# The LRU recurrence in eight half rounds with the heads of the first attention, and the modulation moved

## The reference

```python
mod_x = (silu_c @ w_mod[l] + b_mod[l])        # six vectors of 1024: sh1, sc1, g1, sh2, sc2, g2
px = modulate(rmsnorm(x, g_pre_mix[l]), sh1, sc1) @ w_in[l]        # q, k, v, lx, zx
...
attn_x = latent_attention(group_q(qx), k_all, v_all)               # 8 heads of 64, 1280 keys
yc, yl = rglru_bidir(dwconv(lc, ...), dwconv(lx, ...), ...)        # linear scans, forward and backward
lru_x = yl * jax.nn.gelu(zx)
mix_x = jnp.concatenate([attn_x, lru_x], axis=-1) @ w_out[l]
x_mid = x + g1 * rmsnorm(mix_x, g_post_mix[l])
hx2 = modulate(rmsnorm(x_mid, g_pre_ffn[l]), sh2, sc2)
ffn_x = peer(hx2, ...)                                             # 128 expert rows of u and of v per token
x = x_mid + g2 * rmsnorm(ffn_x, g_post_ffn[l])
```

## Time and profile before

| | us |
|---|---|
| median of 3 runs (3408.39 to 3414.58) | 3409.09 |
| profiled execution | 3407.63 |
| its span | 3405.9 |
| PE, DVE, ACT, POOL busy | 2665.7, 2199.0, 776.0, 1972.8 |

### The profile page before, as it was taken

The page is one execution under the profiler, slowest core; times in us unless marked ns, Lnnn a source line. Parts: engine busy times, 40 slices in busy tenths (PEclk is TensorE's granted clock), DMA queues, the critical chain, the costliest instruction groups (busy, mean ns, idle before and its releaser), DMA issues.

```text
span 3405.9 us, 29441 instructions
## 1 busy us (share of the span) xinstructions
PE 2665.7 (78%) x9084; PEld 1140.6 (33%) x9084; DVE 2199.0 (65%) x4614; ACT 776.0 (23%) x1791; POOL 1972.8 (58%) x2100
## 2 busy tenths in 40 slices
PE   7998768076977897789778977897789777933498
PEld 3775334053233323332333233323332333211122
DVE  2233961899787677767776777677767866766500
ACT  1122432021222132212221222132213221200122
POOL 0000000257677676767777777777777777777775
PEclk9999988578989898889898989898989889967799
DMA  6002340289999999999999999999999999999998
GB/s 237 31 25 81 136 173 13 96 321 393 387 394 407 395 393 395 405 396 391 403 407 398 395 398 407 400 396 393 407 403 402 407 406 396 386 408 408 406 399 356
DMA packets 326923, 1145.15 MB, mean 336 GB/s; under 512 B 37356, under 2 KB 41452, under 8 KB 325623
## 3 DMA queue, kind: packets, MB, share of 16 engines
q0 software_dynamic: 295552, 1075.97, 80.5%
q1 hardware_dynamic: 31224, 67.38, 5.4%
HBM read 1134.83 MB, written 8.39 MB: 336 GB/s over the span
## 4 chain that ended last, share of the span: by engine, by line
PE 40%; DMA 22%; POOL 15%; DVE 14%; issue 7%; ACT 2%; DVEq 0%; SPq 0%; ACTq 0%; POOLq 0%
PE psum L1446 24%; POOL arena L435 15%; DMA arena<-in_v,arena 11%; DMA arena<-in_u,idx_u 10%; DVE arena L1119 5%; PE psum L1401 4%; PE psum L1271 4%; PE psum L1254 2%; PE psum L1328 2%; PE psum L1367 1%; PE psum L1257 1%; PE psum L1380 1%; PE psum L1220 1%; DVE small L992 1%; DMA arena<-in_w_mod 1%
## 5 line engine op out<-in xcount | busy, mean ns | idle before, releaser
L1446 PE MATMUL psum<-arena 128*32 128x512 f32 x4096 | 1369.6, 675 | 328.0 <-DMA arena<-in_v,arena 320.3
L1119 DVE CUSTOM_DVE_ANT_0 arena<-arena,psum 128x1024 f32<-128x1024 f32 x1024 | 1231.8, 1220 | 515.9 <-DMA arena<-in_u,idx_u 485.4
L435 POOL DMA_INDIRECT arena<-in_u,idx_u x1024 | 967.7, 945 | 440.7 <-issue 225.2
L435 POOL DMA_INDIRECT arena<-in_v,arena x1024 | 984.7, 962 | 358.5 <-issue 210.8
L1446 PEld LDWEIGHTS psum<-arena 128*32 128x32 f32 x4096 | 387.0, 119 | 1252.6 <-issue 1073.3
L688 ACT ACTIVATE arena<-arena 128x32 f32<-128x32 f32 x1024 | 316.9, 320 | 1393.8 <-PE psum L1446 1392.3
L1401 PE MATMUL psum<-wbig,arena 128*128 128x512 f32 x512 | 232.5, 609 | 2.2 <-ACT arena L657 2.2
L1328 PE MATMUL psum<-kT,arena 64*128 64x512 f32 (+1 forms) x384 | 176.6, 599 | 59.3 <-ACT arena L619 39.8
L1348 PE MATMUL psum<-ident,arena 128*128 128x128 f32 x640 | 118.3, 310 | 77.4 <-DVE arena L1006 42.1
L1360 PE MATMUL psum<-arena,v 128*64 128x128 f32 x1280 | 161.0, 283 | 22.7 <-ACT arena L630 22.7
L630 ACT ACTIVATE arena<-psum 128x512 f32<-128x512 f32 (+1 forms) x192 | 99.5, 526 | 263.0 <-PE psum L1348 262.7
(11 more groups left out here) (199 smaller groups left out, 2043.9 us busy)
## 6 DMA issues: line engine op xcount, KB each, us to landing
wbig<-in_w_mod SPq DMA_DIRECT2D x8, 2048.0 KB
arena<-in_u,idx_u POOLq DMA_INDIRECT x1024, 6.7
arena<-in_v,arena POOLq DMA_INDIRECT x1024, 6.7
arena<-in_w_mod SPq DMA_DIRECT2D x4, 2048.0 KB, 10.4
wbig<-in_wq SPq DMA_DIRECT2D x1, 8192.0 KB, 35.5
arena<-in_xin SPq DMA_DIRECT2D x5, 1024.0 KB, 5.0
wbig<-in_w_in SPq DMA_DIRECT2D x2, 2048.0 KB, 23.3
arena<-in_w_out SPq DMA_DIRECT2D x1, 4096.0 KB, 15.3
```

Of the source, the lines that this page charges most:

```text
L435: pool.indirect_dma_start(ring[:, r, :], None, t[table], bass.IndirectOffsetOnAxis(idx[:, j:j + 1], 0)).then_inc(got[r], 16)
L1119: V.tensor_tensor_reduce(ring[:, r, :], ring[:, r, :], hx_cur, 1.0, 0.0, ALU.mult, ALU.add, act_[:, j:j + 1]).then_inc(S["u_used"], 1)
L1446: ins = M(bank(4 + b)[QP * q:QP * q + QP, :], lhsT=sel[:, j % SELS, :], rhs=ring[:, r, 512 * b:512 * b + 512], start=(i == 0), stop=(i == ...
```

## The change

Early modulation: four loads of two row blocks by all 2048 columns, issued at once into four places; PE makes the four blocks of 512 columns in the four column groups of 32 (`sil32`), x's transposes in between; one copy, four transposes, `modc`. The clearing by GpSimd stands ahead and only covers pads of XL. w_in is loaded as three tiles (w_kvl, w_q, w_z), the last two after the early matmuls.

Late modulation: during the projections GpSimd loads w_mod in 32 pieces (128 partitions x 2 x 512), scales each with silu(c) and adds it to `acc` (eight blocks of 512 columns). After the projections PE sums `acc` over partitions with ones, in column groups (`mod_sum`), and DVE updates all four rows at once. `acc` lies where the attention's tiles are later, and partly under what ACT and DVE write in the recurrence, so ACT waits for `mod_out`.

The loops of the projections are written out. The constants of the recurrence are computed after pair 0 and the first convolution in the middle of the last pair. SP stores the q tiles.

Recurrence and first attention: round s (0 to 7) has head s and the half round f = s // 2, d = s % 2. a squared, the clamp of b and z squared are ACT's (Square, Relu). Scores are in banks 3 to 5, gates in 0 to 2, one gate at a time, turned probabilities in 6 and 7. cu and hf change places. DVE writes lc for tile 0 itself; the output matmul of tile 0 takes its eight terms in order of their arrival. w_out is loaded after the last `lru_in`.

```diff
+        ATT_AT = ARENA - 4096
+        at[0] = ATT_AT
+        acc = view(8 * 512, 8, 512)
...
+        def score_at(n):
+            return 512 * 3 if isinstance(n, int) and n == 0 else 0
+        def first_pv(h):
+            return bank(6 + h % 2)[0:64, 2 * P:3 * P]
...
-            for n in range(4):
-                if n >= 2:
-                    sp.wait_ge(S["wm_used"], n - 1)
-                sp.dma_start(wm[:, n % 2, :, :], wmv[:, :, 512 * n:512 * n + 512])\
-                    .then_inc(S["wm_loaded%d" % (n % 2)], 16)
+            for i in range(4):
+                dst = (wm_lo, wm_hi)[i // 2][:, 2 * (i % 2):2 * (i % 2) + 2, :]
+                sp.dma_start(dst, wmv[:, 2 * i:2 * i + 2, 0:2 * D]).then_inc(S["wm_loaded%d" % i], 16)
...
+            sp.wait_ge(S["wm_used"], 1)
+            sp.dma_start(w_q, w_inv[:, :, 0:D_ATTN]).then_inc(S["w_q_loaded"], 16)
+            sp.dma_start(w_z, w_inv[:, :, QKV + D_LRU:D_IN]).then_inc(S["w_z_loaded"], 16)
...
+            sp.wait_ge(S["acc_zeroed"], 1)
+            sp.dma_start(acc[0:1, :, :], t["b_mod"][:, 2 * D:6 * D].rearrange("o (i n) -> o i n", i=8))\
+                .then_inc(S["acc_loaded"], 16)
...
+            load_x_pair(2)
+            store_q(0)
+            load_x_pair(3)
+            store_q(1)
+            store_q(2)
+            load_x_pair(4)
+            for x in range(3, NX):
+                store_q(x)
...
+            sp.wait_ge(S["mod_rows"], 1)
+            sp.wait_ge(S["q_stored"], 16 * NX)
+            sp.dma_start(qc, q_scr[0].rearrange("p (j c) -> p j c", j=4)).then_inc(S["q_loaded"], 16)
+            wqv = t["wq"].rearrange("(t p) n -> p t n", p=P)
...
+            sp.dma_start(wq[:, 0:KT - 1, :], wqv[:, 0:KT - 1, :]).then_inc(S["wq_loaded"], 16)
+            for f in range(LF - 1):
+                store_l(f)
+            sp.wait_ge(S["gates_i"], 2 * LF)
+            sp.dma_start(wq[:, KT - 1, :], wqv[:, KT - 1, :]).then_inc(S["wq_last"], 16)
+            sp.wait_ge(S["lru_i"], 2 * LF)
+            sp.dma_start(wo, t["w_out"].rearrange("(t p) n -> p t n", p=P)).then_inc(S["wo_loaded"], 16)
+            store_l(LF - 1)
...
-            pool.wait_ge(S["modc_ready"], 1)
-            pool.wait_ge(S["wm_used"], 4)
-            nc.gpsimd.memset(XL, 0.0).then_inc(S["bd_zeroed"], 1)
...
+            pool.wait_ge(S["modT_ready"], 1)
+            pool.wait_ge(S["acc_loaded"], 16)
+            def stage(i):
+                n, t0 = i // 4, 2 * (i % 4)
+                pool.dma_start(staged[:, i % 2], wml[:, t0:t0 + 2, 512 * (n + 4):512 * (n + 4) + 512])\
+                    .then_inc(S["staged_in%d" % (i % 2)], 16)
+            stage(0)
+            for i in range(32):
+                n, t0 = i // 4, 2 * (i % 4)
+                if i + 1 < 32:
+                    stage(i + 1)
+                pool.wait_ge(S["staged_in%d" % (i % 2)], 16 * (i // 2 + 1))
+                for kt in range(2):
+                    ch.step(nc.gpsimd.tensor_scalar(staged[:, i % 2, kt], staged[:, i % 2, kt],
+                                                    csil[:, 0, t0 + kt:t0 + kt + 1], None, ALU.mult))
+                ch.sync()
+                for kt in range(2):
+                    ch.link(nc.gpsimd.tensor_tensor(acc[:, n, :], acc[:, n, :], staged[:, i % 2, kt], ALU.add))
+            pool.sem_inc(S["mod_summed"], 1)
...
+            def gate_r(k):
+                d = k % 2
+                act.wait_ge(S["gates_r"], k + 1)
+                wait(act, "lru_m", k - 1)
...
+            def gate_a(k):
+                d = k % 2
+                wait(act, "lru_free", k - 1)
+                act.wait_ge(S["r_out"], k + 1)
+                ch.link(A(av[:, d], tr[:, d], ACT.Exp, scale=kcol(k), bias=kcol(k)))
+                A(bv[:, d], av[:, d], ACT.Square)
+                A(tr[:, d], tr[:, d], ACT.Tanh, scale=kcol(k), bias=kcol(k)).then_inc(S["lru_a"], 1)
+            def gate_i(k):
+                d = k % 2
+                act.wait_ge(S["gates_i"], k + 1)
...
+            def lru_root(s):
+                d = s % 2
+                act.wait_ge(S["lru_m"], s + 1)
+                ch.link(A(bv[:, d], bv[:, d], ACT.Relu, scale=-1.0))
+                A(bv[:, d], bv[:, d], ACT.Sqrt, scale=0.25).then_inc(S["lru_s"], 1)
+            def z_square(f):
+                wait(act, "lru_out", f)
+                A(zt, Z[:, f, :], ACT.Square, scale=GELU_C ** 0.5).then_inc(S["z_sq"], 1)
+            def z_tanh(f):
                 act.wait_ge(S["z_in"], f + 1)
-                A(tr[:, 1, 0:SEQ], tr[:, 1, 0:SEQ], ACT.Tanh, scale=GELU_K).then_inc(S["z_tanh"], 1)
-                if f + 1 < LF:
-                    lru_gates(2 * f + 3)
+                A(zt, zt, ACT.Tanh, scale=GELU_K).then_inc(S["z_tanh"], 1)
...
+            gate_r(0)
+            act.wait_ge(S["qkT_ready"], NTOK)
+            act.wait_ge(S["mod_out"], 1)
+            gate_a(0)
+            gate_i(0)
+            probs(0, 0)
+            for s in range(2 * LF):
+                more = s + 1 < 2 * LF
+                lru_root(s)
+                if s % 2:
+                    z_square(s // 2)
+                elif s:
+                    z_tanh(s // 2 - 1)
+                if more:
+                    gate_r(s + 1)
+                move_pT(s, 0)
+                move_pT(s, 1)
+                if more:
+                    gate_a(s + 1)
+                move_pT(s, 2)
+                if more:
+                    gate_i(s + 1)
+                move_pv(s)
+                if more:
+                    probs(0, s + 1)
+            z_tanh(LF - 1)
+            act.wait_ge(S["lru_out"], LF)
...
+                        conv(0)
...
+            def lru_in(k):
+                f, d = k // 2, k % 2
+                dve.wait_ge(S["lru_a"], k + 1)
+                V.scalar_tensor_tensor(bv[:, d], bv[:, d], 1.0, tr[:, d], ALU.add, ALU.mult).then_inc(S["lru_m"], 1)
+                dve.wait_ge(S["i_out"], k + 1)
+                V.scalar_tensor_tensor(ti[:, d], ti[:, d], 1.0, cu(f), ALU.add, ALU.mult).then_inc(S["lru_i"], 1)
+            def lru_scan(s):
+                f, d = s // 2, s % 2
+                a_, b_ = av[:, d], bv[:, d]
+                dve.wait_ge(S["lru_s"], s + 1)
+                dve.wait_ge(S["lru_i"], s + 1)
+                ch.link(V.tensor_tensor(b_, b_, ti[:, d], ALU.mult))
...
+                dve.sem_inc(S["lru_free"], 1)
...
+            def z_in(f):
+                y, zf = hf(f)[:, lx], Z[:, f, :]
+                dve.wait_ge(S["z_sq"], f + 1)
+                V.scalar_tensor_tensor(zt, zt, 1.0, zf, ALU.add, ALU.mult).then_inc(S["z_in"], 1)
+                ch.link(V.tensor_tensor(y, y, hb[:, lx], ALU.add))
+                ch.link(V.scalar_tensor_tensor(y, y, 0.5, zf, ALU.mult, ALU.mult))
+            def z_out(f):
+                y = hf(f)[:, lx]
                 dve.wait_ge(S["z_tanh"], f + 1)
-                ch.link(V.scalar_tensor_tensor(hf[:, lx], zt, 1.0, hf[:, lx], ALU.add, ALU.mult))
+                ch.link(V.scalar_tensor_tensor(lc[:, f, :], zt[:, 0:P], 1.0, y[:, 0:P], ALU.add, ALU.mult))
+                dve.sem_inc(S["lc_first"], 1)
+                ch.link(V.scalar_tensor_tensor(y, zt, 1.0, y, ALU.add, ALU.mult))
...
+            dve.wait_ge(S["mod_rows"], 1)
+            dve.wait_ge(S["gains_loaded"], 48)
+            V.scalar_tensor_tensor(rows[:, :], bank(6, 2), one_a2[:, 0:1], rows[:, :], ALU.add, ALU.mult)\
+                .then_inc(S["mod_out"], 1)
+            lru_in(0)
+            negmax(0, 0)
+            for s in range(2 * LF):
+                more = s + 1 < 2 * LF
+                normalise(0, s)
+                if s and s % 2 == 0:
+                    z_out(s // 2 - 1)
+                lru_scan(s)
+                if more:
+                    negmax(0, s + 1)
+                    lru_in(s + 1)
+                if s % 2:
+                    z_in(s // 2)
+                elif s // 2 + 1 < LF:
+                    conv(s // 2 + 1)
+            z_out(LF - 1)
...
+            for kt in range(KT):
+                if kt % 2 == 0:
+                    pe.wait_ge(S["wm_loaded%d" % (kt // 2)], 16)
+                if kt == 6:
+                    x_transpose(0)
+                for g in range(4):
+                    ins = M(bank(4)[QP * g:QP * g + QP, :], lhsT=sil32[:, kt, :],
+                            rhs=wm(kt)[:, 512 * g:512 * g + 512], start=False, stop=(kt == KT - 1))
+            ins.then_inc(S["wm_used"], 1)
...
+            def gate(k, g):
+                f, d = k // 2, k % 2
+                if g == 0 and d == 0:
+                    pe.wait_ge(S["conv_done"], f + 1)
+                if g:
+                    pe.wait_ge(S["r_out"], k + 1)
+                else:
+                    wait(pe, "i_out", k)
...
+                ins.then_inc(S["gates_i" if g else "gates_r"], 1)
+            def mod_sum():
+                pe.wait_ge(S["mod_summed"], 1)
+                pe.wait_ge(S["lz_out"], LF + 2 * LF * (NTOK // 2 - 1))
+                for i in range(2):
```

(49 more changed lines are left out.)

436 lines of the change are left out of this document (178 added, 258 removed).

## The result

| | before | after |
|---|---|---|
| median of the runs, us | 3408.74 (3407.17 to 3414.58, 4 runs) | 3298.47 (3290.95 to 3304.32, 4 runs) |
| profiled execution, span | 3407.63, 3405.9 | 3295.49, 3293.7 |
| ratio | | 0.9672, 95% interval 0.9648 to 0.9697 |

What follows compares the result with a forecast made beforehand. The prediction took the gathered expert-row stream as the bound behind `route`, and a chain of waits ahead of it. 3407.6 less 14 (early modulation) and 45 (rounds) gave 3349 us, range 3330 to 3384.

Steps and rivals of the forecast that it cites:

- Behind `route`: From the output matmul's end to `route` 49.6 us, and everything behind it, were forecast as unchanged.
- Early modulation: Ahead of the projections: four loads issued at once bring the first LRU matmul from 61.98 to 47.4, 14 us gained.
- The bound of 18 us: Upper bound of the gain ahead of the projections, if the last of the four loads landed at 26.
- Projections: First LRU matmul to the end stays 243 us, with recurrence constants and first convolution, 11.5 us, moved under it.
- GpSimd's sum: Late modulation under the projections: 32 pieces of 4.6 to 6.1 us, ready at 198 to 246, costed at nothing.
- A: Rival: GpSimd's late modulation ends after the projections (291), shifting everything; ready at 321, 30 late, 3379 us; chance 0.08.
- The 19% of the earlier trace: In the projections: a VectorE op took 886 ns with GpSimd idle, 1050 with it active; 2 us in all at most.
- The rounds: Recurrence and first attention interleaved: projections' end to output matmul's end takes 192 us for 237.3, 45 us gained.
- B: Rival: PE's clock stays low through the interleaved rounds, 226 us for 192, 3383 us in all; chance 0.14.
- C: Rival: full clock makes the rounds 182 us and the early part gains 18, 3335 us in all; chance 0.08.
- D: Rival: saved time is waited out in the gather stream, about 3405 us; chance 0.03 together with others.
- Slower by A: Late modulation pieces over 9.3 us make the kernel slower than before; 3446 us at 10.5 per piece; chance 0.05.

Runs made afterwards that it cites:

- b_align: Kernel before with a pad of 32 bytes per partition ahead of the arena, nothing else: 3370.29 us, 0.9880 of the kernel before.
- a_shift: Kernel after with `one_a2` declared behind the arena, so the arena starts where it did before: 3335.39 us, 0.9788 of the kernel before.
- c_after: Kernel after run once more, unchanged, as the measure for later runs on the same chip: 3301.42 us, 0.9679 of the kernel before.
- c_conv: Kernel after with two convolutions in the last pair of the projections, the others in rounds 1 and 3: 3280.15 us, 0.9627 of the kernel before.
- the third set: A set of runs where all kernels, the kernel before too (3727 us), moved their gathered rows at only 355 GB/s.

## Why the prediction was wrong

**Behind `route`: the step that failed.** "From 542.69 to 592.33 and behind it nothing is changed." No instruction was, but the arena had moved by 32 bytes, as the change declares `one_a2` ahead of it (the diff above shows only its use), and each of the 262,144 gathered rows (2 x 1024 gathers of 128) is written to an address in it. This is 34.6 us of the 112.2; b_align and a_shift isolate it at 38 and 37. Without it the kernel after takes 3335.39 us (a_shift), inside the range and 14 us under the forecast. The Trainium skill ("DMA: Bandwidth & Descriptors", How a descriptor splits into AXI transactions) says of what a descriptor reads that a transaction starts only at a 256-byte boundary, so a descriptor that doesn't costs more beats; these rows are written, which it doesn't speak of. By that rule, for 4096 bytes, an estimated 1.6% more at 64 mod 256, 3.1% at 128 and 5.5% at 224 (130, 132 and 135 beats for 128). The sense agrees with the runs, down to the step of 256, and so does the size at 64; at 128 and 224 it doesn't: a packet takes 1.2 to 1.7% more at all three places. That the cause is this split was not tried by itself.

**Early modulation: the mechanism right, the size off**, 21.3 us for 14 (its own terms sum to 14.6). About 2 us of it are the run's: c_after, the same kernel, has its first LRU matmul at 42.77 and not at 40.63. The loads came at 416 and 426 GB/s and not at the 370 taken over from stretches in which they alternated: last landing at 26.6 for 30. The eight matmuls took 1.90 us for 3.4: four groups run side by side, not two. The first qkv matmuls took 5.2 for 5.8. The bound of 18 us had the landing at 26, as it came, and the other terms at the forecast; their 3 us took it past the bound.

**Projections**: 244.6 us for 243, with constants and convolution hidden, as costed.

**GpSimd's sum: cost nothing, as forecast, but on a wrong term.** A piece was bounded by 4.6 and 6.1 us and took 7.2 (from the first issue at 51.55 to 283.49, 32 pieces). The scaling, 1669 ns, was costed like a copy, at 0.90 us; that is the term that failed. The addition, 1305, lay in its bounds. Slack was 3.9 us and not 45 to 90, so that the chance of A was worth more than it was given. By the figures of the Trainium skill ("GPSIMD Engine Reference", section 3.1) a piece was an estimated 4.7 us; the trace says 7.2, and the scaling is 2.2 times the 769 ns that the page has for 512 elements in its best case. The other statement of the page (section 8, Key points) is that the engines contend where VectorE has two SBUF inputs or is in a 2-port perf mode. For two inputs the trace agrees with 783 for 416 ns, but has 680 for 684 beside it; which operations ran in such a mode no trace shows. The 19% of the earlier trace rows was no bound: there GpSimd only issued, and beside its arithmetic an operation of the same kind (L891) took 2.3 times as long.

**The rounds: the mechanism right, the size off**, 56.6 us for 45. To the end of the first exponential 15.5 us for 24.3: the sum over partitions is eight matmuls, the prediction counted 16, and it cost each at 0.56 us; it took 1.90 and not 9.0. Pairs of rounds took 37.2, 40.4 and 40.7 for 39.7, 41.5 and 41.4, seven steps 134.9 for 141.4; even rounds were shorter than forecast (15.7 for 17.7, then 16.7 for 18.8) and the later odd ones longer (21.5 for 22.0, then 23.8 and 24.0 for 22.7). The granted clock was 0.83 for the 0.77 taken. The end 13.3 for 12.1; w_out did release the output matmul (issued at 436.26, 12.6 us to landing), as forecast. The output matmul took 16.9 for 14.0, partly at the low clock. ACT is the busiest engine, at 77% of the window; over 80% was forecast.

**The rivals.** B didn't come: the granted clock of the rounds was 0.83, above the 0.77 of the forecast. C gave 182 and 18 together, 3335, and a_shift, the change without the new place, takes 3335.39. That is luck: C's mechanism was a full clock, which didn't come, and the 180.7 us came from the shorter sum over partitions and the shorter even rounds instead. D is excluded: c_conv's saving passed whole within the spread. Slower by A needed a piece of 9.3 us, 1.5 times the upper bound (the 1.7 of the prediction belongs to its 10.5 us); it took 7.2.

What stays open: why 64, 128 and 224 mod 256 cost alike, what slowed the rows in the third set, and why the place cost less there.
